# The last six x tiles transposed by DMA, and the loads of the convolution moved behind x

## The chip, the cores and the metric

The kernel runs on the 8 cores of one Trainium2 chip, the same program on each core with its own data. Time is in device microseconds (us) of the slowest core. A core has the engines TensorE (PE), VectorE (DVE), ScalarE (ACT), GpSimd (POOL) and SyncE (SP), and 16 DMA engines. DMAs are issued here from SP (queue q1 of the profile) and from POOL (queue q0).

## The reference, cut to what matters

One layer of a hybrid convolutional decoder, for 8 prompt sequences of 2048 tokens and 128 short sample sequences of 8 tokens; a core gets one prompt sequence and 16 samples, 2176 tokens in all.

```
u = rmsnorm(h) * g_mix
a_b, a_c, a_h, a_z, b_v, b_g, b_z, gate_a, gate_b = split(u @ w_in)      # 9 blocks of 1024 columns
ya = (a_b * dwconv3(a_c * a_h) * silu(a_z)) @ w_out_a
v  = b_v * sigmoid(b_g)
c  = dwconv31(history ++ v) + bias                                       # samples carry 30 rows of history
yb = (silu(layernorm(c)) * silu(b_z)) @ w_out_b
h  = h + (sigmoid(gate_a) * ya + sigmoid(gate_b) * yb) @ w_o
h  = h + sigmoid(rmsnorm(h) * g_ple @ w_pg) * (p @ w_pe)
y  = rmsnorm(h) * g_final
```

## The kernel before, in words

Each engine's instruction stream is written out by hand: `Sched.add` takes an operation with what it reads and writes and puts it at the end of its engine's stream; semaphore waits follow from the reads and writes. So an engine, and a DMA queue's issuer too, goes through its list in program order, and an operation whose input is late holds up all that stand behind it. `pdma` issues a DMA from POOL (it can cast f32 to bf16) and lets six be under way: the seventh waits until the first has landed. `sdma` issues from SP.

Stage 1 brings x in as 17 tiles of 128 tokens (tile index 0 is the samples, 1 to 16 the prompt; six buffers `x1`, four buffers `xb1`). For a tile `s1_a1` squares and sums a row on ACT (its unused product goes into `xb1`) and makes the factor `rsd` with two small operations on POOL; `s1_a2` scales the tile into `xb1` on ACT (line 484); `s1_b` turns it by 8 PE transposes into PSUM (line 498) and copies that on DVE, times g_mix, into `uT` (line 503). Step i of `s1_step` is `s1_b(i)`, `s1_a2(i+1)`, `s1_a1(i+2)`.

Stage 2 is woven with it: `s2_proj(j, si, o, n)` computes channel block j of the GLU for n tokens from `uT` (16 matmuls, line 409; sigmoid on ACT, line 528; product on DVE, line 535) and stores v rows to the DRAM scratch `vd`. The list `PIECES` runs blocks j = 0 to 3 over pieces of the tokens; the flags of a piece say after which j a step of stage 1 stands. The last piece, (3, 0, 512), reads tiles 13 to 16; the piece (2, 256, 256) reads tiles 11 and 12. After the last piece the eight weight buffers (`ring`) come free pair by pair, and POOL loads the weights of j = 4 to 7 into them. Blocks 4 to 7 then run as 20 jobs, the first being j = 4 on the samples.

Between those jobs stand the 16 halves of the convolution (`conv_half`, 20 matmuls each, line 604; halves 2j and 2j+1 belong to block j). A half needs its weights `Wp`, built on DVE from the taps `tw` and a `mask` (`w_build`, line 588), and the window `v8`: prompt rows loaded back from `vd` (`conv_load`, on SP), the history of the samples (`hist_load`, on POOL, one load per j) and their new rows (`vs_load` from `vsd`, then a DVE copy in `conv_samples`, line 580). `v8` has two buffers, so `conv_load(j + 2)` waits for the second half of j.

The rest (branch A, the output projections, the merge, and the per-tile stage 6 with its DMA transposes on SP, line 860) is not changed, except for `s6_tail`, which computes the last two tiles in pieces: `sig` (ACT, line 936) writes the gate into buffer `B`, `comb` (DVE) multiplies and adds, `sqr` (ACT, line 954) squares and sums into the unused half of `yt`, `out` scales and stores.

Of the kernel before, what the change touches and what calls it, by code (L numbers as in the profile page):

```python
# [7 lines left out]
F32 = mybir.dt.float32  # L8
# [4 lines left out]
D = 1024  # L13
# [143 lines left out]
def build_program():  # L157
# [11 lines left out]
    h8_d = din("h8", [NCH, 128, NQ, 80])  # L169
# [10 lines left out]
    gple_d = din("gple", [128, D])  # L180
    gfin_d = din("gfin", [128, D])
# [12 lines left out]
    with contextlib.ExitStack() as st:  # L194
# [50 lines left out]
        wo_t = at("wo_t", [128, NCH, D], BF16, o_acc)  # L245
        NRING = 8
# [41 lines left out]
        xb1 = [at(f"xb1{i}", [128, D], BF16, o_r4 + 4096 * NXS + 2048 * i) for i in range(NXB)]  # L288
        X1_RES = [f"x1{i}" for i in range(NXS)] + [f"xb1{h}{i}" for i in range(NXB) for h in ("", "h")]
# [149 lines left out]

        xnext = [0]  # L440
# [49 lines left out]
        def s1_b(i):  # L490
            t = TILES[i]
# [417 lines left out]
        def s6_tail(t):  # L909
# [3 lines left out]
            gb, eb, cc = {}, {}, {}  # L913

# [18 lines left out]
            def sig(t, i):  # L933
                (o, n), b, x = parts[t][i], gb[t, i], t % 2
                rs_ap, rs_res = s6[t]
                S.add("act", lambda e: e.activation(out=B[x][:, o:o + n], in_=ps[:, b, 0:n], func=AF.Sigmoid, scale=rs_ap),
                      reads=[f"ps{b}", rs_res], writes=[f"B{x}h{i}"])

            def comb(t, i):
                (o, n), b, x, w = parts[t][i], eb[t, parts[t][i][0] // 512], t % 2, t % 4  # L940
                S.add("dve", lambda e: e.tensor_tensor(out=B[x][:, o:o + n], in0=ps[:, b, o % 512:o % 512 + n],
                                                       in1=B[x][:, o:o + n], op=ALU.mult),
                      reads=[f"ps{b}", f"B{x}h{i}"], writes=[f"B{x}h{i}"])
                S.add("dve", lambda e: e.tensor_tensor(out=B[x][:, o:o + n], in0=B[x][:, o:o + n], in1=A[w][:, o:o + n],
                                                       op=ALU.add),
                      reads=[f"B{x}h{i}", f"A{w}"], writes=[f"B{x}h{i}"])

            def sqr(t, i):
                (o, n), x = parts[t][i], t % 2
                if t not in cc:  # L950
# [3 lines left out]
                S.add("act", lambda e: e.activation(out=yt[x][:, o:o + n], in_=B[x][:, o:o + n], func=AF.Square,  # L954
                                                    accum_out=ssq[:, c:c + 1]),
                      reads=[f"B{x}h{i}"], writes=[f"yt{x}h{i}", f"ssq{c}"])
# [9 lines left out]
            def out(t):  # L966
                x, c = t % 2, cc[t] + len(parts[t]) - 1
                for h in range(2):
# [18 lines left out]
            halves_of(ta % 2)  # L987
# [8 lines left out]
            halves_of(tb % 2)  # L996
# [23 lines left out]
        def s1_step():  # L1020
            i = nxt[0]
            if i < len(TILES):
                nxt[0] += 1
                s1_b(i)
                s1_a2(i + 1)
                s1_a1(i + 2)
# [20 lines left out]
        for f, i in FIRST:  # L1047
# [4 lines left out]
            else:  # L1052
# [3 lines left out]
        PIECES += [(1, 0, 256, (1, 0, 1, 0)), (1, 256, 256, (1, 1, 1, 0)), (2, 0, 256, (1, 1, 0, 1)),  # L1056
                   (2, 256, 256, (1, 0, 1, 0)), (3, 0, 512, (0, 0, 0, 0))]
        builds = [(0, 0), (0, 1), (1, 0)]
        for p, (si, o, n, prep) in enumerate(PIECES):
            for j in range(4):  # L1060
# [7 lines left out]
                if si == 3 and o == 0 and builds:  # L1068
                    w_build(*builds.pop(0))
                if si == 2 and o == 0 and j < 2:  # L1070
                    hist_load(j)
                    vs_load(j)
            if p == 0:
# [8 lines left out]
                sdma(hista[:], sa_d, [], ["hista"], "hista")  # L1082
        S.alias([f"cq{q}_{g}" for q in range(4, 8) for g in range(NQ)] + [f"c{q}_4" for q in range(4, 8)], X1_RES)

# [54 lines left out]
        conv_samples(7)  # L1139
        s3_job(0, 3)  # L1140
# [181 lines left out]
```

How the kernel before makes its waits and increments, by code:

```python
            def run(engname, e):  # L113
                waited = {}
                for o in ops:
                    if o["eng"] != engname:
                        continue
                    need = {}
                    for d in o["deps"]:
                        od = ops[d]
                        v = od["seq"] * (16 if od["dma"] is not None else 1)
                        if v > need.get(od["chan"], 0):
                            need[od["chan"]] = v
                    for c, v in need.items():
                        if waited.get(c, 0) >= v:
                            continue
                        e.wait_ge(sems[c], v)
                        waited[c] = v
                    ins = o["fn"](e)
                    if o["signal"]:
                        ins.then_inc(sems[o["chan"]], 16 if o["dma"] is not None else 1)
                if engname == final_wait_eng:
                    for c, v in final.items():
                        if waited.get(c, 0) < v:
                            e.wait_ge(sems[c], v)
```

## Time and profile before

| | |
|---|---|
| median of 3 runs | 882.98 us (882.97 to 884.48) |
| the profiled execution: its time, and the span from first to last instruction on the slowest core | 885.41 us, 882.6 us |
| spans of the 8 cores | 877.8 to 882.6 us |
| mean granted TensorE clock, by core | 0.992 to 0.995 of full speed |
| busy share of the span: PE, DVE, ACT, POOL | 97%, 58%, 34%, 16% |

The profile is of the slowest core, number 3. Busy time of PE is modelled from pipelined matmuls, so a gap in it is read from the start times of groups. Times of events are from the start of the span.

### The profile page before, as it was taken

The numbers are of one execution on the slowest core, as the hardware profiler recorded it, in microseconds if no ns is written. First come the engines' busy times: TensorE is split into PE (matmuls) and PEld (weight loads), VectorE is DVE, ScalarE is ACT, GpSimd is POOL, SyncE is SP. The second block draws the span as 40 slices with busy tenths as digits, with TensorE's granted clock in tenths as the row PEclk, the third lists the DMA queues.
The fourth block names the chain that finished last, engine by engine and source line by source line (L and its number), as shares of the span: only waits on it lengthen the run. The fifth ranks groups of instructions, "written<-read, shape, count | busy, mean of one in ns | idle before, by whom it ended". The sixth has DMA issues, their size and how long they took to land.

```text
span 882.4 us, 15282 instructions; the slowest of 8 cores (877.8 to 882.6 us)
## 1 busy us (share of the span) xinstructions
PE 854.6 (97%) x4970; PEld 441.6 (50%) x4970; DVE 509.0 (58%) x794; ACT 301.9 (34%) x568; POOL 146.1 (17%) x275
## 2 busy tenths in 40 slices
PE   7999999999999999999999999999999999999993
PEld 4886555555454444454454544444444444444441
DVE  2455234576997777777677732333233325777775
ACT  4773224355443232423323321111111112444443
POOL 3242101100101101020110101110001001344442
PEclk9999999999999999999999999999999999999997
DMA  9987899996203213030413276522222145766642
GB/s 190 258 154 98 160 184 176 151 155 116 49 1 48 38 24 61 13 61 1 61 15 59 33 147 96 86 38 46 49 49 33 22 83 129 196 182 170 172 127 98
DMA packets 94108, 84.42 MB, mean 96 GB/s; under 512 B 53296, under 2 KB 74800, under 8 KB 93488
## 3 DMA queue, kind: packets, MB, share of 16 engines
q0 software_dynamic: 27776, 31.17, 25.3%
q1 hardware_dynamic: 66256, 52.29, 24.9%
q8 instruction: 41, 0.67, 0.3%
q14 instruction: 35, 0.29, 0.1%
HBM read 86.80 MB, written 15.61 MB: 116 GB/s over the span
## 4 chain that ended last, share of the span: by engine, by line
PE 85%; DMA 7%; issue 2%; DVE 2%; ACT 2%; POOL 1%; DVEq 0%; POOLq 0%; SPq 0%; ACTq 0%
PE ps L409 65%; PE ps L849 7%; PE ps L870 6%; PE ps L604 4%; DMA t_v<-vd 3%; DMA t_x<-x 2%; PE ps L876 1%; DMA vd<-t_vrow 1%; PE ps L672 1%; DMA t_ring<-w_in 1%; ACT t_xb L424 1%; ACT t_xb L484 1%; DVE t_tmp L714 1%; PE ps L498 0%; PE ps L919 0%
## 5 line engine op out<-in xcount | busy, mean ns | idle before, releaser
L409 PE MATMUL ps<-t_uT,t_ring 128*128 128x512 bf16 (+2 forms) x3200 | 542.6, 329 | 1.5 <-DMA t_ring<-w_in 0.7
L409 PEld LDWEIGHTS ps<-t_uT,t_ring 128*128 128x128 bf16 x3200 | 278.2, 98 | 253.5 <-issue 4.3
L823 DVE TENSOR_TENSOR t_tmp<-ps,t_tmp 128x512 f32<-128x512 f32 (+1 forms) x80 | 48.7, 611 | 151.2 <-PE ps L409 150.6
L343 POOL DMA_DIRECT2D t_ring<-w_in x72 | 39.0, 543 | 391.2 <-PE ps L409 388.3
L820 ACT ACTIVATE t_tmp<-ps 128x512 f32<-128x512 f32 (+1 forms) x80 | 42.3, 532 | 177.2 <-PE ps L409 177.2
L781 ACT ACTIVATE t_tmp<-t_tmp,t_vid 128x512 f32<-128x512 f32 (+1 forms) x40 | 30.0, 749 | 124.0 <-DVE t_tmp L778 124.0
L535 DVE TENSOR_TENSOR t_vrow<-ps,t_tmp 128x512 bf16<-128x512 f32 (+2 forms) x52 | 25.2, 485 | 80.8 <-PE ps L409 38.1
L409 PE MATMUL ps<-t_cb,t_ring 128*128 128x512 bf16 (+1 forms) x320 | 65.4, 347 | 0.0
L409 PE MATMUL ps<-t_yaT,t_ring 128*128 128x512 bf16 (+1 forms) x320 | 65.4, 347 | 0.0
L849 PE MATMUL ps<-t_wo_t,t_cb 128*128 128x512 bf16 x272 | 61.5, 379 | 0.0
L870 PE MATMUL ps<-t_wpg_t,t_u2T 128*128 128x512 bf16 x240 | 54.3, 379 | 0.0
L604 PE MATMUL ps<-t_v,t_Wp 128*128 128x336 bf16 x320 | 48.0, 306 | 4.3 <-DMA t_v<-vd 3.3
L714 DVE SCALAR_TENSOR_TENSOR t_tmp<-t_sx,t_vid,t_tmp 128x512 f32<-128x512 f32 x64 | 48.1, 751 | 6.7
L426 POOL TENSOR_SCALAR t_msq<-t_ssq 128x1 f32<-128x1 f32 x49 | 22.7, 464 | 132.5 <-ACT t_yt L424 50.0
L409 PEld LDWEIGHTS ps<-t_yaT,t_ring 128*128 128x128 bf16 x320 | 29.0, 98 | 30.2
L409 PEld LDWEIGHTS ps<-t_cb,t_ring 128*128 128x128 bf16 x320 | 28.9, 98 | 30.2 <-issue 0.3
L743 DVE TENSOR_TENSOR t_sx<-ps,t_tmp 128x512 f32<-128x512 f32 x32 | 22.1, 690 | 36.1 <-ACT t_tmp L735 31.6
L849 PEld LDWEIGHTS ps<-t_wo_t,t_cb 128*128 128x128 bf16 x272 | 26.6, 98 | 31.8
L604 PEld LDWEIGHTS ps<-t_v,t_Wp 128*128 128x128 bf16 x320 | 31.0, 98 | 21.2 <-issue 5.6
L870 PEld LDWEIGHTS ps<-t_wpg_t,t_u2T 128*128 128x128 bf16 x240 | 23.5, 98 | 28.3
L528 ACT ACTIVATE t_tmp<-ps 128x128 f32<-128x128 f32 (+2 forms) x60 | 23.4, 405 | 36.5 <-PE ps L409 36.3
L611 ACT ACTIVATE t_c<-ps 128x512 f32<-128x512 f32 x32 | 19.0, 596 | 46.2 <-PE ps L604 46.2
(99 smaller groups left out, 764.1 us busy)
## 6 DMA issues: line engine op xcount, KB each, us to landing
t_ring<-w_in POOLq DMA_DIRECT2D x72, 256.0 KB, 6.5
t_x<-x SPq DMA_DIRECT2D x17, 512.0 KB, 8.8
t_xs<-x SPq DMA_DIRECT2D x17, 512.0 KB, 4.7
t_cb<-t_c SPq DMA_DIRECT2D x64, 128.0 KB, 5.1
y<-t_yt SPq DMA_DIRECT2D x15, 512.0 KB, 3.2
vd<-t_vrow SPq DMA_DIRECT2D x28, 128.0 KB, 5.4
t_v<-vd SPq DMA_DIRECT2D x7, 512.0 KB, 7.0
t_ring<-w_oa POOLq DMA_DIRECT2D x8, 256.0 KB, 8.0
```

Of the source, the lines that this page charges most:

```text
L343: S.add("pool", lambda e: e.dma_start(out=out, in_=in_), reads=reads, writes=list(writes) + [swq()], dma=key)
L409: S.add("pe", lambda e, k=k: e.matmul(ps[:, b, 0:n], lhsT=ring[k_ring][:, k, :], rhs=rhs_fn(k), start=(k == 0), stop=(k == NCH - 1)), read ...
L426: S.add("pool", lambda e: e.tensor_scalar(out=msq[:, c:c + 1], in0=ssq[:, c:c + 1], scalar1=1.0 / D, scalar2=EPS, op0=ALU.mult, op1=ALU.ad ...
L528: S.add("act", lambda e: e.activation(out=tmp[tg][:, 0:n], in_=ps[:, bg, 0:n], func=AF.Sigmoid), reads=[f"ps{bg}"], writes=[f"tmp{tg}"])
L535: S.add("dve", lambda e: e.tensor_tensor(out=vst[q][:, o:o + n], in0=ps[:, bv, 0:n], in1=tmp[tg][:, 0:n], op=ALU.mult), reads=[f"ps{bv}", ...
L604: S.add("pe", lambda e, b=b, qq=qq, q=q, d=d: e.matmul(ps[:, b, 0:NWIN], lhsT=Wp[w][:, qq * NLAG + d, :], rhs=v8[s][:, q, 4 - d:4 - d + NWIN],
L714: S.add("dve", lambda e, k=k: e.scalar_tensor_tensor(out=tmp[t2][:, 0:n], in0=tp[k], scalar=vecs[:, V_WCA + 3 * j + k:V_WCA + 3 * j + k + ...
L781: S.add("act", lambda e: e.activation(out=tmp[tx][:, 0:n], in_=tmp[tx][:, 0:n], func=AF.Silu, scale=vcol(V_LNG, j), bias=vcol(V_LNB, j)), ...
L820: S.add("act", lambda e, p=p, t=t: e.activation(out=tmp[t][:, 0:n], in_=ps[:, p, 0:n], func=AF.Sigmoid), reads=[f"ps{p}"], writes=[f"tmp{t}"])
L823: S.add("dve", lambda e, p=p, t=t: e.tensor_tensor(out=tmp[t][:, 0:n], in0=ps[:, p, 0:n], in1=tmp[t][:, 0:n], op=ALU.mult), reads=[f"ps{p} ...
L849: S.add("pe", lambda e, h=h, b=b, k=k: e.matmul(ps[:, b, :], lhsT=cbb[:, k, mcol:mcol + 128], rhs=wo_t[:, k, 512 * h:512 * h + 512], start ...
L870: S.add("pe", lambda e, h=h, b=b, k=k: e.matmul(ps[:, b, :], lhsT=u2T[t % 3][:, k, :], rhs=wpg_t[:, k, 512 * h:512 * h + 512], start=(k == ...
```

## The change

Tiles 11 to 16 of x are no longer turned by PE: DVE scales them with `rsd` and with g_mix (a new input, held as a full row tile `gmix` in the space of the later sums) into `xb1`, and a DMA transpose from SP writes `uT`. For the other tiles stage 1 stays. The sample stores, `mask` and `tw` leave the first piece and stand on POOL behind the fourth; the histories of all j come in one load of 1 MB (after the cast) into `hst`, issued just ahead of them, and `conv_samples` copies a block's part into `v8` on DVE. `hst` lies partly under the `xb1` buffers 1 to 3 (`HST_UNDER`), so its load waits for their last transposes. The steps of stage 1 move forward by some blocks. In the tail the last tile gets other buffers for `B` and for the squares.

```diff
+        FIRST_DT = 11
...
         def s1_a2(i):
...
+            if i >= FIRST_DT:
+                t = TILES[i]
+                si, o = t // 4, 128 * (t % 4)
+                S.add("dve", lambda e: e.scalar_tensor_tensor(
+                    out=xb1[bq][:], in0=xs1[xq][:], scalar=rs_ap, in1=gmix[:], op0=ALU.mult, op1=ALU.mult),
+                    reads=[f"x1{xq}", rs_res, "gmix"], writes=[f"xb1{bq}", f"xb1h{bq}"])
+                if xnext[0] < len(TILES):
+                    s1_load(xnext[0])
+                S.add("sp", lambda e: e.dma_start_transpose(out=uT[si][:, :, o:o + 128], in_=xb1[bq][:]),
+                      reads=[f"xb1{bq}", f"xb1h{bq}"], writes=[f"uT{t}", f"uTh{t}"], dma=f"uT{bq}")
+                return
...
+            if i == 6:
+                sdma(gmix[:], gmix_d, [], ["gmix"], "gmix")
 
         def s1_b(i):
+            if i >= FIRST_DT:
+                return
...
-        def hist_load(j):
-            s = j % 2
-            pdma(v8[s][:, :, 260:340], h8_d[j], [], [f"v8{s}h"], f"v8{s}h")
+        def hist_load():
+            S.alias(["hst"], HST_UNDER)
+            pdma(hst.rearrange("p j q s b -> p (j q s b)"), h8_d, [], ["hst"], "hst")
 
         def conv_load(j):
             s = j % 2
-            if j >= 2:
-                hist_load(j)
...
         def conv_samples(j):
             s = j % 2
+            S.add("dve", lambda e: e.tensor_copy(
+                out=v8[s][:, :, 260:340].rearrange("p q (s b) -> p q s b", b=5)[:, :, :, 0:4], in_=hst[:, j]),
+                reads=["hst"], writes=[f"v8{s}h"])
...
+            qb, qj = tb % 3, (tb + 1) % 3
+            Bt = {ta: (B[ta % 2], f"B{ta % 2}"), tb: (xs[qb], f"xs{qb}")}
+            junk = {ta: (yt[ta % 2], f"yt{ta % 2}"), tb: (xs[qj], f"xs{qj}")}
...
-        PIECES += [(1, 0, 256, (1, 0, 1, 0)), (1, 256, 256, (1, 1, 1, 0)), (2, 0, 256, (1, 1, 0, 1)),
-                   (2, 256, 256, (1, 0, 1, 0)), (3, 0, 512, (0, 0, 0, 0))]
+        PIECES += [(1, 0, 256, (1, 0, 1, 0)), (1, 256, 256, (1, 1, 1, 1)), (2, 0, 256, (1, 1, 1, 0)),
+                   (2, 256, 256, (0, 0, 0, 0)), (3, 0, 512, (0, 0, 0, 0))]
...
-                if si == 3 and o == 0 and builds:
+                if si == 3 and j > 0 and builds:
                     w_build(*builds.pop(0))
-                if si == 2 and o == 0 and j < 2:
-                    hist_load(j)
+                if si == 3 and 1 <= j < 3:
+                    j -= 1
                     vs_load(j)
+            if p == 3:
+                hist_load()
+            if p == 3:
+                for j in range(4):
+                    vsd_store(j)
+                pdma(mask[:], mask_d, [], ["mask"], "mask")
+                pdma(tw.rearrange("p a b -> p (a b)"), tw_d, [], ["tw"], "tw")
             if p == 0:
...
-                for j in range(4):
-                    vsd_store(j)
-                pdma(mask[:], mask_d, [], ["mask"], "mask")
-                pdma(tw.rearrange("p a b -> p (a b)"), tw_d, [], ["tw"], "tw")
                 sdma(hista[:], sa_d, [], ["hista"], "hista")
...
-        h8 = hist.reshape(16, 5, NPH, NCH, NQ, 16).transpose(3, 5, 2, 4, 0, 1)
-        m["h8"] = f(h8.reshape(NCH, 128, NQ, 80))
+        h8 = hist[:, 0:32].reshape(16, 4, NPH, NCH, NQ, 16).transpose(5, 2, 3, 4, 0, 1)
+        m["h8"] = f(h8.reshape(128, NCH * NQ * 64))
```

## Rows read from the trace of the kernel before

**Rows 1.** Busy time by stretch (us, PE, PEld, DVE, ACT, POOL, PEclk, DMA share, GB/s).

```profile
55.00:73.00 18.00, 17.07 (x177) 15.18 (x178) 9.83 (x22) 13.43 (x25) 5.53 (x12) 1.00 0.75 92
...
120.00:127.00 7.00, 4.42 (x20) 2.50 (x20) 2.16 (x3) 0.69 (x2) 0.00 (x0) 0.76 1.55 141
...
206.00:860.00 654.00, 653.71 (x3444) 314.01 (x3442) 401.69 (x600) 199.18 (x352) 100.78 (x177) 1.00 0.36 73
```

**Rows 2.** Timeline of PE, 52 to 97 us (start us, us, what, idle before).

```profile
52.67 1.91 PE L409 MATMUL ps<-t_uT,t_ring 128*128 128x256 bf16 x16
...
61.96 0.61 PE L498 MATMUL ps<-t_idb,t_xb 128*128 128x128 bf16 x8 [0.47 <-ACT t_xb L484]
62.40 3.66 PE L409 MATMUL ps<-t_uT,t_ring 128*128 128x256 bf16 x32
...
72.90 23.52 PE L409 MATMUL ps<-t_uT,t_ring 128*128 128x256 bf16 x128
```

**Rows 3.** Timeline of PE, the three convolution halves that waited.

```profile
97.30 3.02 PE L604 MATMUL ps<-t_v,t_Wp 128*128 128x336 bf16 x20 [0.88 <-DMA t_v<-vd]
...
122.72 4.65 PE L604 MATMUL ps<-t_v,t_Wp 128*128 128x336 bf16 x20 [2.58 <-DMA t_v<-vd]
...
172.06 3.02 PE L604 MATMUL ps<-t_v,t_Wp 128*128 128x336 bf16 x20 [0.99 <-DVE t_vkeep_s L549]
```

**Rows 4.** Timeline of ACT in the tail.

```profile
868.70 1.42 ACT L936 ACTIVATE t_B<-ps,t_rsd 128x512 f32<-128x512 f32 x3 [0.58 <-DVE t_yt L904]
871.32 0.63 ACT L954 ACTIVATE t_yt<-t_B 128x512 f32<-128x512 f32 x1 [1.20 <-DMA y<-t_yt]
```

**Rows 5.** Groups of DVE by line and shape, 20 to 80 us.

```profile
L503 DVE TENSOR_TENSOR t_uT<-ps,t_vid 128x1024 bf16<-128x1024 bf16 x14 | 17.0, 1217 | 0.1
```

**Rows 6.** Timeline of DVE and of POOL, 849 to 853 us.

```profile
851.05 1.28 DVE L904 SCALAR_TENSOR_TENSOR t_yt<-t_B,t_rsd,t_gfin 128x1024 f32<-128x1024 f32 x1
...
849.47 0.18 POOL L426 TENSOR_SCALAR t_msq<-t_ssq 128x1 f32<-128x1 f32 x1 [3.28 <-ACT t_yt L424]
...
851.19 1.19 POOL L426 TENSOR_SCALAR t_msq<-t_ssq 128x1 f32<-128x1 f32 x1 [0.83 <-ACT t_xs L424]
```

**Rows 7.** Line 860, the DMA transposes of stage 6.

```profile
L860 SPq DMA_TRANSPOSE t_u2T<-t_xb x17: 1222/1224/1351, 734.6 to 859.0; - x17
...
DMA to landing us min/median/max: 2.8/2.8/4.6
```

**Rows 8.** Page, DMA issues of x (KB each, median us to landing).

```profile
t_x<-x SPq DMA_DIRECT2D x17, 512.0 KB, 8.7
```

**Rows 9.** Timeline of POOL, 49 to 78 us.

```profile
49.58 2.19 POOL L343 DMA_DIRECT2D vsd<-t_vkeep_s  x4
...
77.16 0.62 POOL L343 DMA_DIRECT2D t_ring<-w_in  x1 [6.68 <-PE ps L409]
```

**Rows 10.** DMA view, 690 to 740 us (KB each, median us to landing).

```profile
t_wpg_t<-w_pg POOLq DMA_DIRECT2D x2, 1024.0 KB, 13.0
```

**Rows 11.** DMA view, 48 to 53 us.

```profile
t_tw<-tw POOLq DMA_DIRECT2D x1, 640.0 KB, 10.3
```

**Rows 12.** DMA view, 76 to 78 us.

```profile
t_ring<-w_in POOLq DMA_DIRECT2D x1, 256.0 KB, 4.0
```

**Rows 13.** DMA view, 83 to 86 us.

```profile
t_ring<-w_in POOLq DMA_DIRECT2D x2, 256.0 KB, 8.7
t_v<-vd SPq DMA_DIRECT2D x1, 512.0 KB, 12.1
```

**Rows 14.** DMA view, 63 to 70 us (packets, MB, share of 16 engines).

```profile
q0 software_dynamic: 1805, 0.29, 61.7%
...
t_v<-h POOLq DMA_DIRECT2D x2, 160.0 KB, 4.2
```

**Rows 15.** DMA view, 109 to 110 us.

```profile
t_v<-vd SPq DMA_DIRECT2D x1, 512.0 KB, 13.1
```

**Rows 16.** Timeline of DVE, 171 to 172 us.

```profile
171.57 0.34 DVE L580 COPY t_v<-t_vs 128x128 bf16<-128x128 bf16 x1
```

More of the change, by code:

```diff
@@ L168, in build_program @@
     sa_d = din("sa", [128, NCH, 32])
-    h8_d = din("h8", [NCH, 128, NQ, 80])
+    h8_d = din("h8", [128, NCH * NQ * 64])
     sbh_d = din("sbh", [352, D])
@@ L180, in build_program @@
     gple_d = din("gple", [128, D])
+    gmix_d = din("gmix", [128, D])
     gfin_d = din("gfin", [128, D])
@@ L245, in build_program @@
         wo_t = at("wo_t", [128, NCH, D], BF16, o_acc)
+        gmix = at("gmix", [128, D], F32, o_acc)
         NRING = 8
@@ L288, in build_program @@
         xb1 = [at(f"xb1{i}", [128, D], BF16, o_r4 + 4096 * NXS + 2048 * i) for i in range(NXB)]
+        hst = at("hst", [128, NCH, NQ, 16, 4], BF16, o_cb + NCH * NTOK * 4 - NCH * NQ * 128)
+        assert o_cb + NCH * NTOK * 4 - NCH * NQ * 128 >= o_r4 + 4096 * NXS + 2048
+        HST_UNDER = [f"xb1{h}{i}" for i in range(1, NXB) for h in ("", "h")]
         X1_RES = [f"x1{i}" for i in range(NXS)] + [f"xb1{h}{i}" for i in range(NXB) for h in ("", "h")]
@@ L953, in sqr @@
                 c, last = cc[t] + i, i == len(parts[t]) - 1
-                S.add("act", lambda e: e.activation(out=yt[x][:, o:o + n], in_=B[x][:, o:o + n], func=AF.Square,
+                S.add("act", lambda e: e.activation(out=jt[:, o:o + n], in_=bt[:, o:o + n], func=AF.Square,
                                                     accum_out=ssq[:, c:c + 1]),
-                      reads=[f"B{x}h{i}"], writes=[f"yt{x}h{i}", f"ssq{c}"])
+                      reads=[f"{br}h{i}"], writes=[f"{jr}h{i}", f"ssq{c}"])
                 S.add("pool", lambda e: e.tensor_scalar(
@@ L971, in out, with halves_of @@
                     S.add("dve", lambda e, hs=hs: e.scalar_tensor_tensor(
-                        out=yt[x][:, hs], in0=B[x][:, hs], scalar=rsd[:, c:c + 1], in1=gfin[:, hs],
+                        out=yt[x][:, hs], in0=bt[:, hs], scalar=rsd[:, c:c + 1], in1=gfin[:, hs],
                         op0=ALU.mult, op1=ALU.mult),
-                        reads=[f"B{x}h{i}" for i in ii] + [f"rsd{c}", "gfin"], writes=[f"yt{x}h{i}" for i in ii])
+                        reads=[f"{br}h{i}" for i in ii] + [f"rsd{c}", "gfin"], writes=[f"yt{x}h{i}" for i in ii])
                     sdma(y_d[128 * t:128 * t + 128, hs], yt[x][:, hs], [f"yt{x}h{i}" for i in ii], [], f"yl{t % 2}{h}")
-            def halves_of(x):
-                S.alias([f"B{x}h{i}" for i in range(3)], [f"B{x}"])
-                S.alias([f"yt{x}h{i}" for i in range(3)], [f"yt{x}"])
+            def halves_of(*names):
+                for nm in names:
+                    S.alias([f"{nm}h{i}" for i in range(3)], [nm])
             gates(ta, 0)
@@ L986, in s6_tail @@
             gates(tb, 1)
-            halves_of(ta % 2)
+            halves_of(f"B{ta % 2}", f"yt{ta % 2}", f"xs{qb}", f"xs{qj}")
             sig(ta, 0)
@@ L995, in s6_tail @@
             s6_out(ta - 1)
-            halves_of(tb % 2)
+            halves_of(f"yt{tb % 2}")
             sqr(ta, 0)
@@ L1021, in s1_step @@
             i = nxt[0]
[L1022 to L1026, printed above, removed]
+            nxt[0] += 1
+            s1_b(i)
+            s1_a2(i + 1)
+            s1_a1(i + 2)
         def s1_load5():
@@ L1077, in build_program @@
                     S.add("pool", lambda e, i=i: e.memset(v8[i][:, :, 0:4], 0.0), writes=[f"v8{i}z"])
-                for j in range(4):
-                    vsd_store(j)
-                pdma(mask[:], mask_d, [], ["mask"], "mask")
-                pdma(tw.rearrange("p a b -> p (a b)"), tw_d, [], ["tw"], "tw")
                 sdma(hista[:], sa_d, [], ["hista"], "hista")
+        assert nxt[0] == len(TILES) - 1
         S.alias([f"cq{q}_{g}" for q in range(4, 8) for g in range(NQ)] + [f"c{q}_4" for q in range(4, 8)], X1_RES)
+        S.alias([f"acc{c}{si}" for c in "sq" for si in range(5)], ["gmix"])
         jobs = [(j, si) for j in range(4, 8) for si in (4, 0, 1, 2, 3)]
@@ L1139, in build_program @@
         conv_samples(7)
+        S.alias([f"cq7_{g}" for g in range(NQ)] + ["c7_4"], ["hst"])
         s3_job(0, 3)
@@ L1275 @@
     shared = dict(w_in=cols(w_in[0]), w_oa=cols(w_out_a[0]), w_ob=cols(w_out_b[0]), w_o=rows(w_o[0]),
-                  w_pg=rows(w_pg[0]), w_pe=rows(w_pe[0]), tw=tw, mask=mask, vecs=vecs, gfin=gfin, gple=gple)
+                  w_pg=rows(w_pg[0]), w_pe=rows(w_pe[0]), tw=tw, mask=mask, vecs=vecs, gfin=gfin, gple=gple, gmix=gmix)
     def phases(a):
```

23 lines of the change are left out of this document (12 added, 11 removed).

## The prediction

> **What bounds the kernel now.** I read the busy time by stretch first, then PE's own timeline, then the DMA view of the stretches where PE stands still. From 206 to 860 us PE is busy 653.71 of 654 us [rows 1], and the change touches nothing there. So the change can only work before 206 us, and in the tail.
>
> Up to 73 us PE loses time to stage 1. Between 52.67 and 72.90 it runs nine blocks of 16 matmuls; two blocks in a row last 3.66 us and one 1.91, so a further one costs 1.75 and nine cost 15.75 [rows 2]. The other 4.5 us of the 20.2 are the transposes of tiles 11 to 16 (0.61 us each, of which some 0.15 overlaps the next block) and the gaps ahead of them, such as the 0.47 us in which PE waits for ACT's scaling [rows 2]. The piece (3, 0, 512) starts at 72.90 + 1.75 = 74.65.
>
> From 97 to 206 us PE waits three times [rows 3]: at 97.30 (0.88 us, half 0, its prompt rows from `vd`), at 122.72 (2.58 us, half 4, the same load of j = 2) and at 172.06 (0.99 us, half 10, behind DVE). The second wait costs more than it lasts: its 20 matmuls take 4.65 us where 20 others take 3.02, and the stretch 120 to 127 us has a granted clock of 0.76 [rows 1, 3], which means that part of it ran at 1.2 instead of 2.4 GHz, after PE had stood still. The shorter two cost no clock. The DMA engines are fully taken there: their share is 1.55 [rows 1].
>
> **Part 1, transposes: 4.5 us.** PE loses 48 transposes and no longer waits for them, if `uT` is there in time. DVE trades six copies of 1.217 us [rows 5] for six scalings of two f32 rows into bf16; the nearest row, the same operation at the same size, has 1.28 [rows 6]: +0.4 us in all, hidden since DVE is busy 9.83 of 18 us there [rows 1]. ACT loses six scalings and its loop with POOL. The new chain is square (ACT), two POOL operations, scaling (DVE), transpose (SP). DVE does one scaling and one block's product per step, estimated at 1.9 us a step, from about 54 us: tile 10's copy, 1.2 us [rows 5], begins when its transposes end, at 52.7. The six scalings then end at 55.9, 57.8, 59.7, 61.6, 63.5 and 65.4. A transpose lands 2.8 us after its issue, at most 4.6 [rows 7]; it occupies SP for 1.22 us, and only stores of v stand behind it there, for which nobody waits yet. Tile 12 is there at 60.6 and needed at 52.67 + 6 x 1.75 = 63.2; tile 16 is there at 68.2 and needed at 63.2 + 7.0 = 70.2. The squares of tiles 15 and 16 wait for the transposes of 11 and 12 (one `xb1` buffer); these land at 58.7 and 60.6, in time for scalings at 61.6 and 63.5. So the last piece starts at 70.2 instead of 74.65. With the landing at 4.6 throughout, tile 16 comes some 1 to 2 us late; the gain is between 2.5 and 4.5 us, and I take 4.5, as the median of 17 transposes is the lowest of them.
>
> One detail: the POOL operation that makes a factor took 0.18 us alone and 1.19 us when it started under a 1.28 us DVE scaling of the same kind [rows 6]. The Trainium skill has a rule for this (SBUF — State Buffer, section "Who interferes with whom"): a DVE operation with two SBUF inputs and a GpSimd operation that reads SBUF share a port pair, and the second waits for the whole of the first. By it each new scaling can put up to 1.2 us into the next tile's chain; the trace agrees. All of it in one tile would use up 1.2 of the 2 us that tile 16 has to spare, so the sum stays and only the chance of late transposes grows.
>
> **Part 2, POOL's queue before the last piece.** Leaving the first piece, the four sample stores free POOL of 2.19 us [rows 9]. They, `mask` and `tw` now stand behind `hist_load`, which waits for tile 15's transpose, about 66.3 us. Two loads of 1 MB issued together land after 13.0 us [rows 10]: 6.1 us per MB and about 1.3 more. So `hst` lands at 66.3 + 7.4 = 73.7. `tw` is the seventh POOL DMA and waits for it; 640 KB make 5.1 us at that pace, against 10.3 measured with x traffic beside it [rows 11]: 79 to 84. Behind `tw` stand the weights of j = 4. Two of 256 KB take 3.2 us at that pace, so they land at about 82 to 87. PE wants them at 70.2 plus four blocks of twice 1.75, which is 84.2. Before, the first was issued at 77.16 and landed in 4.0 us [rows 9, 12], 7 us before PE came. I take no wait, since x is over by then and the idle-queue pace is nearer; at the other end PE waits 3 us and loses some 1.6 us of clock. DVE also stands at the first `w_build` until `tw` lands; behind it are two blocks' products, and PE has free PSUM banks for two jobs more.
>
> **Part 3, half 0: -0.6 us.** PE would come to half 0 two such blocks and a quarter later, at 92.1. Its prompt rows are stored after block (3, j = 0), now 4.5 us earlier; before, the load came 12.1 us after its issue, beside weight loads that took 8.7 [rows 13]. The same eight weight loads run beside it now, and `vs_load(0)` has moved behind it on SP's queue, and the DVE copy behind that. I take a wait of 1.5 us in place of 0.88: bounds 0 and 3 us.
>
> **Part 4, half 4: +3.8 us.** Two history loads of 0.29 MB in total, 1805 packets, take 61.7% of 16 engines over 7 us [rows 14]: 2.2 us each. One such load stood on POOL just ahead of, and another behind, the load of `vd` for j = 2, which landed after 13.1 us [rows 15]. Without the first it should land some 2.2 us sooner. The wait of 2.58 shrinks to 0.4, like those that cost no clock, and the 1.63 us of slow matmuls go too: 2.2 + 1.6 = 3.8. Bounds: 0, if SP's issue and the stores are what delays the load, and 4.2.
>
> **Part 5, half 10: -0.6 us.** DVE's sample copy ends at 171.9, just before PE goes on at 172.06 [rows 3, 16]. Ahead of it now stands the history copy: 512 elements a partition, between 0.34 us (the copy of 128, [rows 16]) and 1.217 (1024 elements, [rows 5]). I take 0.6, all of it on PE's path. The other seven copies lie beside DVE idle time.
>
> **Part 6, tail: +0.5 us.** The last tile's gate waits 0.58 us for DVE to read the shared `B`, and its square waits 1.20 for the store of `yt` [rows 4]. With other buffers ACT starts the gate when its previous square ends, 0.5 us sooner, and DVE's chain behind it moves along; the second wait lies within the same stretch and brings no more. Bounds 0.3 and 0.8.
>
> **The sum.** 4.5 - 0.6 + 3.8 - 0.6 + 0.5 = 7.6 us. The profiled execution took 885.41 us, with a span of 882.6; the runs' median is 882.98, 2.4 us less, and I take the sum from it: **875.4 us**.
>
> **Rivals.**
> *The weights come late* (the other side: slower). `hst` and `tw` stand ahead of the weights of j = 4. At the slowest rows for each step, `hst` 13.0, `tw` 10.3, weights 8.7 us [rows 10, 11, 13], they land at 66.3 + 32.0 = 98.3 instead of 84.2. PE then waits 14.1 us and loses 1.6 of clock; half 0's extra wait vanishes. 875.4 + 15.7 - 0.6 gives 890.5. It decides against the change from a landing at about 91 us on, when the wait has eaten the 7.6 us. For it: six DMAs at once, and some 1.8 MB ahead of the weights that were not there before. Against it: those rows all had other traffic beside them.
> *The transposes come late.* In this stage x took 8.7 us to land [rows 8]. With that for a transpose, tile 12 comes at 66.5 (3.3 us late), tile 16's square waits for it, its scaling ends about 70 and it lands about 78.8: the last piece starts 8.6 us later than I say, and the clock may fall by another 1.6: 884 to 885.6 us. Against: the 17 transposes of stage 6, with loads of x and stores of y beside them, needed 4.6 at most [rows 7].
> *Half 4 still waits.* If the load of j = 2 is held by SP's stores and not by histories, part 4 is 0: 879.2.
> *All waits go:* 4.5 + 0.9 + 4.2 + 1.0 + 0.6 = 11.2 us: 871.8.
>
> **Chances.** Forecast, within 2.5 us of 875.4: 0.50. Half 4 still waits, or a wait of 2 to 4 us at the weights (878 to 881): 0.22. All waits go: 0.08. Weights late enough to lose all: 0.10. Transposes late: 0.10, of which half ends between 880 and 884. A measurement of this kernel can tell 0.2% (1.8 us) from no change. Faster 0.80, same 0.08, slower 0.12. The range is 871.5 to 882.5; the two late cases lie mostly outside.
>
> **What would show it.** After: no transposes of PE behind 53 us, the last piece near 70 us; j = 4's first job near 84 with no wait on `ring`; half 0 near 93; half 4 with a wait under 1 us and 3.0 us long; half 10 with a wait of 1.6; ACT's gate of the last tile right behind the square. The prediction is wrong if PE waits on `uT` at 63 or 70 us, or on `ring` at 84, or if half 4's rows still land after 13 us.

## The result, and the profile after

The changed kernel took 894.28 us (median of 4 runs, 893.91 to 895.24), the kernel before 883.73 us on the same chip (4 runs): a ratio of 1.012, 95% interval 1.010 to 1.0139. It is slower, by some 10.6 us; 875.4 was forecast. The profiled execution took 893.91 us, with a span of 892.4 on core 0, its slowest; the rows of before are core 3's, its slowest.

PE's timeline on core 0 (start us, us, what, idle ahead of it and what ended it), beside [rows 2] and [rows 3]:

```profile
53.05 17.63 PE L415 MATMUL ps<-t_uT,t_ring 128*128 128x256 bf16 x160
70.98 13.76 PE L415 MATMUL ps<-t_uT,t_ring 128*128 128x512 bf16 x62 [0.30 <-issue]
94.41 1.01 PE L415 MATMUL ps<-t_uT,t_ring 128*128 128x128 bf16 x8 [9.67 <-DMA t_ring<-w_in]
96.93 9.53 PE L415 MATMUL ps<-t_uT,t_ring 128*128 128x128 bf16 x39 [1.50 <-DMA t_ring<-w_in]
109.48 3.02 PE L628 MATMUL ps<-t_v,t_Wp 128*128 128x336 bf16 x20 [3.03 <-DVE t_v L604]
...
132.16 3.02 PE L628 MATMUL ps<-t_v,t_Wp 128*128 128x336 bf16 x20
...
180.53 3.02 PE L628 MATMUL ps<-t_v,t_Wp 128*128 128x336 bf16 x20 [1.66 <-DVE t_vkeep_s L572]
```

Behind 53 us no transposes are left on PE, and the last piece starts at 70.98. Then PE stands for 9.67 and 1.50 us, until the weights of j = 4 land, and for 3.03 us ahead of half 0, which begins at 109.48 where it began at 97.30. Half 4 has no wait left, half 10 waits 1.66 us.

POOL's timeline (its DMA issues, core 0) shows what the weights stood behind:

```profile
69.95 0.60 POOL L349 DMA_DIRECT2D t_hst<-h  x1 [5.20 <-DVE t_vkeep L564]
70.55 2.12 POOL L349 DMA_DIRECT2D vsd<-t_vkeep_s  x4
72.66 0.54 POOL L349 DMA_DIRECT2D t_mask<-mask  x1
82.54 0.54 POOL L349 DMA_DIRECT2D t_tw<-tw  x1 [9.34 <-DMA t_hst<-h]
83.10 2.74 POOL L349 DMA_DIRECT2D t_ring<-w_in  x5
92.01 0.53 POOL L349 DMA_DIRECT2D t_ring<-w_in  x1 [6.17 <-DMA t_tw<-tw]
```

`tw` is the seventh transfer and waits 9.34 us for the histories; the weights, first issued at 77.16 before [rows 9], are issued at 83.10. The DMA view of 82 to 86 us (KB each, median us to landing), beside [rows 12] and [rows 13]:

```profile
t_ring<-w_in POOLq DMA_DIRECT2D x5, 256.0 KB, 14.6
t_tw<-tw POOLq DMA_DIRECT2D x1, 640.0 KB, 8.9
t_v<-vd SPq DMA_DIRECT2D x1, 512.0 KB, 23.2
...
t_vs<-vsd SPq DMA_DIRECT2D x1, 32.0 KB, 24.8
```

The five weight loads took 14.6 us in the median (before, the first alone took 4.0 and the two of 83 us 8.7); the first two of them, for which PE stood, landed 11.1 and 12.9 us after their issue. The prompt rows took 23.2 us (12.1 before), and 32 KB of sample rows, behind them on SP's queue, 24.8. What fills the DMA engines shows in the busy time by stretch, first the kernel before, then the changed one, both on core 0 (us, PE, PEld, DVE, ACT, POOL, PEclk, DMA share, GB/s):

```profile
56.00:72.00 16.00, 15.25 (x157) 13.44 (x155) 9.13 (x19) 12.14 (x22) 5.55 (x12) 1.00 0.79 98
72.00:84.00 12.00, 11.95 (x75) 6.87 (x75) 6.42 (x13) 2.31 (x6) 2.22 (x4) 1.00 0.48 81
84.00:98.00 14.00, 12.78 (x70) 6.14 (x70) 4.75 (x10) 2.67 (x5) 2.66 (x5) 1.00 0.97 168
```

```profile
56.00:72.00 16.00, 15.70 (x140) 13.53 (x139) 10.64 (x25) 6.39 (x15) 5.87 (x12) 1.00 0.94 144
72.00:84.00 12.00, 11.95 (x57) 5.46 (x56) 1.53 (x4) 2.39 (x4) 2.61 (x6) 1.00 0.85 124
84.00:98.00 14.00, 2.83 (x21) 1.89 (x20) 5.64 (x7) 0.28 (x1) 3.36 (x7) 0.62 0.93 144
```

Before, the DMA engines had room (0.79, 0.48) until 84 us; now they have none from 56 us on. PE's granted clock was 0.62 from 84 to 98 us, where it mostly stood. From 56 to 72 us SP's queue alone, which carries the transposes, held them for 91.0% of the time, where it held 16.6% before:

```profile
q1 hardware_dynamic: 7091, 2.26, 91.0%
```

That is 14.6 us against 2.7. Six stores of v were issued there instead of three; if these take the 2.7 us twice, some 9 us are left for six transposes, 1.5 us of all 16 engines each (an estimate). With nothing beside it a transpose takes less: one of stage 6, in the kernel before, held them for 83.0% of the 1.4 us from 735.7 to 737.1, which is 1.16 us. The landing of the six, beside [rows 7]:

```profile
DMA to landing us min/median/max: 3.1/3.8/5.8
```

### The profile page after: what moved, and what is told of

It reads as the page before. It is cut to its first block, busy times and chain, and to the rows that moved or that the text cites. A ratio compares the mean times of both kernels' runs of the same rounds, so it can differ in the third digit from the quotient of the medians.

```text
span 892.4 us, 15095 instructions; the slowest of 8 cores (886.1 to 892.4 us)
## 1 busy us (share of the span) xinstructions
PE 848.8 (95%) x4841; PEld 439.9 (49%) x4922; DVE 511.7 (57%) x802; ACT 296.4 (33%) x562; POOL 137.7 (15%) x268
## 4 chain that ended last, share of the span: by engine, by line
PE 87%; DMA 8%; issue 2%; DVE 1%; ACT 1%; POOL 0%; DVEq 0%; SPq 0%; POOLq 0%; ACTq 0%
PE ps L415 67%; PE ps L873 7%; PE ps L894 6%; PE ps L628 5%; DMA t_vs<-vsd 3%; DMA t_x<-x 3%; DMA t_ring<-w_in 1%; PE ps L900 1%; DMA vd<-t_vrow 1%; PE ps L696 1%; PE ps L946 0%; ACT t_xb L430 0%; PE ps L521 0%; DVE t_accs L667 0%; DVE t_B L968 0%
```

## The experiments

Each ran beside the kernel before on the same chip. Theory A: the order on POOL's queue (`hst`, then `tw`, then the weights) makes the loss. Rivals: B, the megabyte of histories alone; C, the DMA transposes alone; then D and E, that the DMA engines' time runs out. This table is the result in short: ratio to the kernel before, then from PE's timelines the smallest and the largest wait over the eight cores, in us.

| kernel | ratio (95%) | PE waits for transposes | for weights of j = 4 | at half 0 |
|---|---|---|---|---|
| before | 1 | 0 | 0 | 0 to 2.3 |
| changed | 1.0120 (1.0100 to 1.0139) | 0 | 4.5 to 11.2 | 2.4 to 5.1 |
| e1 stores, tw early | 1.0048 (1.0031 to 1.0066) | 2.1 to 4.6 | 0 | 4.3 to 6.6 |
| e2 e1, histories behind weights | 1.0113 (1.0097 to 1.0129) | 1.3 to 2.6 | 0 | 9.4 to 11.1 |
| e3 old histories, stores early | 1.0032 (1.0003 to 1.0060) | 3.6 to 6.2 | 0 | 0 to 0.9 |
| e4 old histories, stores late | 1.0059 (1.0041 to 1.0078) | 2.8 to 6.1 | 0 | 3.5 to 4.9 |
| e5 no DMA transposes | 1.0111 (1.0060 to 1.0163) | 0 | 3.7 to 7.5 | 2.5 to 5.1 |
| e6 histories, tw split | 1.0089 (1.0056 to 1.0121) | 0 to 2.6 | 0 to 4.1 | 5.5 to 14.9 |
| e7 e2, sample rows early | 1.0093 (1.0065 to 1.0121) | 1.4 to 5.4 | 0 | 7.9 to 10.9 |
| e8 tail alone | 0.9989 (0.9967 to 1.0010) | 0 | 0 | 0 to 1.6 |
| e9 before plus 1 MB | 1.0028 (1.0000 to 1.0055) | 0 | 0 | 2.2 to 3.9 |
| e10 one load in conv stretch | 1.0034 (1.0014 to 1.0055) | 0 | 0 | 0 to 4.6 |
| e11 e10, three DMA transposes | 1.0066 (1.0041 to 1.0091) | 2.0 to 4.2 | 0 | 0 to 7.8 |
| e12 e7, no histories | 1.0008 (0.9992 to 1.0024) | 1.6 to 6.0 | 0 | 0 to 2.3 |
| e13 tw ahead of histories | 1.0191 (1.0139 to 1.0243) | 1.1 to 21.2 | 0 to 3.8 | 0.3 to 5.9 |
| e14 small loads | 0.9993 (0.9958 to 1.0028) | 0 to 6.7 | 0 | 0 to 2.5 |
| e15 e14, no DMA transposes | 1.0013 (0.9993 to 1.0033) | 0 | 0 | 0 to 3.9 |
| e16 e14, four DMA transposes | 1.0066 (1.0041 to 1.0092) | 1.2 to 4.7 | 0 | 0 to 3.4 |

### What held the weights: e5, e1, e13

**e5.** All tiles on TensorE again, with the steps of before and without the load of the gain; the rest as changed.

```diff
-        FIRST_DT = 11
+        FIRST_DT = 99
```

> Edit: the changed kernel with all tiles of x transposed on TensorE as before, and without the load of the broadcast gain; the one load of the histories, the late stores, mask and tw, and the tail stay. Theory A (the order on POOL's queue alone sets the loss): the histories land some 12 us after their issue, tw and the weights of j = 4 follow as in the changed kernel, PE waits about 10 us for them, and the 4 us of TensorE's transposes come back on top: 892 to 898 us. Theory D (the time of the 16 DMA engines is what runs out between 56 and 98 us; the queue that carries the transposes holds 91% of them from 56 to 72 us, where the same queue before held 17%): without the transposes the histories land in 8 to 9 us, PE waits 2 to 4 us: 878 to 886 us.

1.0111: as slow as the changed kernel. On core 4:

```profile
73.33 15.72 PE L415 MATMUL ps<-t_uT,t_ring 128*128 128x256 bf16 x80
93.19 0.61 PE L415 MATMUL ps<-t_uT,t_ring 128*128 128x128 bf16 x8 [4.14 <-DMA t_ring<-w_in]
96.34 9.76 PE L415 MATMUL ps<-t_uT,t_ring 128*128 128x128 bf16 x40 [2.54 <-DMA t_ring<-w_in]
```

The first row begins with one block of the piece before (1.75 us), so the last piece starts at 75.08, 4.1 us later than the 70.98 with DMA transposes; the histories were issued at 70.89 us, as in the changed kernel (69.95). Over the eight cores PE asks for the first weights 3.7 us later on average (88.4 against 84.7) and begins with them only 1.1 us later (91.8 against 90.8). So most of what PE gains is waited away, the two times can't be told apart, and rival C falls for this wait. The time is theory A's, the length of the wait is between A and D. The histories took 9.7 to 11.8 us to land, and 10.1 to 12.0 in the changed kernel: without the DMA transposes they were hardly faster.

**e1.** The stores, `mask` and `tw` back behind piece 0.

```diff
             if p == 3:
                 hist_load()
-            if p == 3:
-                for j in range(4):
-                    vsd_store(j)
-                (mask, tw)
             if p == 0:
+                for j in range(4):
+                    vsd_store(j)
+                (mask, tw)
```

> Edit: the changed kernel with the four vsd stores, mask and tw back behind piece 0, ahead of the rest of x; the 1 MB of histories stays where the change puts it, ahead of the last piece. Theory A (tw, held until the histories have landed by the six transfers that POOL may have in flight, holds the weights of j = 4 behind it): the five weight loads are issued from about 75 us, share the queue with the histories, and PE's wait at 84 to 85 us falls from 11.2 us to about 4 or less; 880 to 886 us. Rival B (the megabyte of histories alone delays the weights): hardly less wait, 889 to 894 us. Rival C (the DMA transposes and what SP carries set it): no change, 892 to 895 us.

PE's wait for weights is gone on all cores, with the megabyte still ahead of them. Part of that is hidden, though. The first of the weights landed at 85.3 to 88.4 us (80.3 to 82.5 before, 86.3 to 94.2 in the changed kernel), and PE, itself held by the transposes, asked later; at the changed kernel's 84.7 it would have waited some 1 to 4 us (an estimate). That much is left to rival B, the megabyte alone; the rest of the 4.5 to 11.2 us is not. The time, 889.45 us, is above theory A's range: some 40% of the loss stays, in two new places (core 3):

```profile
66.48 31.56 PE L415 MATMUL ps<-t_uT,t_ring 128*128 128x256 bf16 x176 [3.09 <-DMA t_uT<-t_xb]
...
103.97 5.76 PE L628 MATMUL ps<-t_v,t_Wp 128*128 128x336 bf16 x20 [5.93 <-DVE t_v L604]
```

The transposes come 3.09 us late, and half 0 waits 5.93 us for DVE's copy of sample rows.

**e13.** `tw` ahead of the histories, nothing else.

```diff
-            if p == 3:
-                hist_load()
             if p == 3:
                 for j in range(4):
                     vsd_store(j)
                 (mask, tw)
+                hist_load()
```

> Edit: the changed kernel with the load of all histories behind the four stores, mask and tw, still ahead of the last piece: an exchange of places on POOL's queue and nothing else. If the order alone made the wait (tw held until the histories have landed, and the weights behind tw): tw lands some 9 us after 73 us, and PE's wait for the weights of j = 4 falls from 4.5 to 11.2 us to under 4 us on every core; 882 to 889 us. If the bytes set it, whatever their order: the wait stays over 4 us on most cores, 891 us or more.

The wait for weights fell to 3.8 us and less, as the order alone should do; on two cores, where PE came far too late to need them, that shows nothing, on the other six it does. The time did not fall: 1.0191, the slowest of all. On two cores the last transposes, beside which `tw` and then the histories were issued, came 16.0 and 21.2 us late. Line 499 (the transposes) on one of them, who waited for it and the landing:

```profile
  PE ps L415: 21.2, 1
...
DMA to landing us min/median/max: 3.1/4.7/23.8
```

So theory A names the cause of most of this wait: the same bytes in the other order leave 0 to 3.8 us of it, the histories without `tw` beside them (e1) some 1 to 4, and `tw` late without the histories (e4, below) had the first weights there by 81.7 to 85.0 us. Its cure moves the wait to another transfer.

### What held half 0: e2, e7, e6, e12, e9

**e2.** As e1, with the histories behind the first weights.

```diff
                 if si == 3 and o + n == 512:
                     wdone(s2w[j][0])
+                if si == 3 and j == 0:
+                    hist_load()
```

> Edit: as the experiment with the stores early, and the load of the histories stands behind the first weight loads of j = 4 (after the first job of the last piece). Theory A and rival B both expect that the weights land before PE asks at 84 to 85 us and the wait there is under 1 us: 875 to 880 us, the first conv half may still wait for sample rows up to 3 us. Rival C: still 887 to 895 us.

A clear miss for all: no wait for weights, but 9.4 to 11.1 us at half 0. The DMA view of core 7, 80 to 90 us:

```profile
q0 software_dynamic: 359, 1.16, 87.4%
q1 hardware_dynamic: 140, 0.13, 4.7%
```

POOL's queue has 87.4% of the DMA engines, SP's 4.7%. On SP's stand the stores of v that the rows of half 0 are loaded from (10.3 us to landing in this stretch), then those rows, then the sample rows, for which DVE waits until 108.34.

**e7.** As e2, with `vs_load` at the third piece, as before.

```diff
-                if si == 3 and 1 <= j < 3:
-                    j -= 1
+                if si == 2 and o == 0 and j < 2:
                     vs_load(j)
```

> Edit: as the experiment with the histories behind the weights, and the two loads of sample rows back where the kernel before has them, at the third column piece instead of behind the first load of conv rows. If half 0 waited there for the sample rows alone (19 us to landing behind 512 KB of conv rows): its wait of 9.6 to 11 us falls to 0 to 3 us, 885 to 889 us, the rest of the loss being the transposes that come late (1.3 to 2.6 us on the slow cores) and what follows them. If the histories themselves or the DMA engines' time hold half 0: 892 us or more.

No better: half 0 now waits for the prompt rows themselves, which on core 2 took

```profile
t_v<-vd SPq DMA_DIRECT2D x1, 512.0 KB, 21.2
```

**e6.** A quarter of the histories and of `tw` ahead of the last piece, the rest behind it and behind half 0; both `vs_load` ahead of the first `conv_load`.

```diff
             if p == 3:
-                hist_load()
+                hist_load(0)      # j = 0, 1
...
-                pdma(tw.rearrange("p a b -> p (a b)"), tw_d, [], ["tw"], "tw")
+                tw_load(0)        # j = 0, 1
...
+                if si == 3 and j == 3:
+                    tw_load(1)
...
                 half()
+                if hk[0] == 1:
+                    hist_load(1)
```

> Edit: the changed kernel with the histories of j = 0, 1 (256 KB) ahead of the last piece and the other 768 KB behind the first conv half, tw's part for j = 0, 1 (160 KB) ahead of the last piece and its other 480 KB behind it, and both early loads of sample rows ahead of the first load of conv rows. Theories A and D: 1.2 MB fewer stand ahead of the weights of j = 4; PE's waits at 84 and at 94 us fall to under 2 us together and half 0 waits under 1 us: 873 to 880 us, under both kernels. Where the transposes then come late instead, as in the experiment with the old histories: 882 to 888 us.

A miss too. The weights were nearly in time, the rows of half 0 were not (5.5 to 14.9 us): `vs_load` waits on SP's queue for the late sample stores, and the prompt rows behind it leave later, into the rest of `tw` and the histories.

**e12.** As e7, the histories' tile set to zero instead of loaded, so that their part is missing from the output.

```diff
-            pdma(hst.rearrange("p j q s b -> p (j q s b)"), h8_d, [], ["hst"], "hst")
+            S.add("dve", lambda e: e.memset(hst.rearrange("p j q s b -> p (j q s b)"), 0.0), writes=["hst"])
```

> Edit: as the experiment with the histories behind the weights and the sample rows early, but the histories are not loaded: VectorE sets their tile to zero, so the output lacks their part. Theory E: PE's wait of 8 to 11 us at half 0 falls to under 2 us and the waits for the transposes (1.4 to 5.4 us) stay: 880 to 886 us. If half 0 waits for something else: 891 us or more.

Half 0 waits 0 to 2.3 us instead of 7.9 to 10.9, and the prompt rows take

```profile
t_v<-vd SPq DMA_DIRECT2D x1, 512.0 KB, 14.0
```

on core 2; over the eight cores 7.7 to 14.0 us, against 15.3 to 21.2 in e7. So in e7 the megabyte held them; it cost 0.85% (1.0093 against 1.0008), 7.5 us, give or take 3. Without any history load the kernel is still no faster than before, as the transposes are 1.6 to 6.0 us late.

**e9.** The kernel before with that megabyte added, unread.

```diff
+            if p == 3:
+                hst_load()
```

> Edit: the kernel before with one load added, the megabyte of histories ahead of the last column piece, whose data nothing reads (the histories by j stay and are used). Theory E (the DMA engines' time between the last piece and the first conv half is full: 2 MB of weights and the 512 KB of conv rows fill 97% of it from 84 to 98 us already, and the large packets of POOL's queue take it ahead of SP's): the weights of j = 4 land some 4 us later and the conv rows of half 0 8 to 10 us later; 6 to 11 us slower than before. Theory A in its narrow form (only tw, held until the histories have landed, delayed the weights, and nothing is held here): up to 3 us slower.

0.28%, 2.5 us (0 to 4.9): theory E's price, 6 to 11 us, is wrong for this place, and only its direction is right. Issued at 71 us, into a stretch in which the DMA engines of the kernel before have a share of 0.48, the megabyte landed after 13.1 us (core 6) and cost half 0 about 2 us. The same megabyte costs some three times that behind the weights (e7). Bytes alone don't set the price; what they run beside does, and e7 differs from e9 in more than the place, as its transposes go by DMA.

### What made the transposes late: e3, e4, e14 to e16, e11

**e3.** Only the transposes and the tail; histories, stores, `tw` and sample rows as before.

> Edit: the transposes by DMA and the buffers of the last tile alone; histories by j in the conv stretch, stores, mask and tw early, sample rows at the third column piece, all as in the kernel before. Theory A and rival B: the forecast's terms for half 4 (3.8) and half 10 (0.6) are lost and the rest stays: about 879 to 881 us. Rival C: 887 to 895 us.

1.0032, not faster: PE waits 3.6 to 6.2 us for the transposes, more than the 4 us that they save. From 50 to 56 us all of `tw` is issued (landing 11.5 us), from 56 to 72 two history loads of small packets, and a transpose's landing goes from 3.8 to

```profile
t_uT<-t_xb SPq DMA_TRANSPOSE x5, 5.0
```

as the median of five on core 5, 9.4 at most. The time, 888.5 us, misses what A and B promised and lies in rival C's range: the DMA transposes alone, in the old order, lose what they should gain. With the landings beside it, this is theory D.

**e4.** The changed kernel with the old histories, stores and `tw` still late.

> Edit: the changed kernel with the histories by j in the conv stretch as before, no load of all histories; the four vsd stores, mask and tw stay late, ahead of the last piece. Theory A: tw is issued at about 73 us without the histories to wait for, the weights of j = 4 some 3 to 5 us later than with early stores, PE waits 0 to 4 us: 879 to 885 us. Rival B: as the experiment with the old histories, 879 to 881 us. Rival C: 890 us or more. If instead the late tw alone were enough for the loss, 888 us or more.

1.0059, above theory A's range. No wait for weights, so late `tw` alone does not make it; the transposes are late by 2.8 to 6.1 us, with the small-packet history loads and the stores beside them and `tw` only from 71 us on (they land after 6.0 us in the median on core 0), and half 0 waits 3.5 to 4.9 us for sample rows.

**e14, e15, e16.** Early: stores, `mask`, a quarter of `tw`, sample rows; histories of j = 0, 1 ahead of the last piece; later 128 KB of histories and 80 KB of `tw` for each j. e15 has no DMA transposes, e16 four.

```diff
         def conv_load(j):
+            if j >= 2:
+                hist_load(j, j + 1)
+                if j + 2 < NCH:
+                    tw_load(j + 2, j + 3)
...
             if p == 3:
-                hist_load()
+                hist_load(0, 2)
...
+                if si == 3 and j == 3:
+                    tw_load(2, 4)
```

> Edit: six transposes by DMA and the tail's buffers; stores, mask and a quarter of tw (160 KB) early, sample rows early, the histories of j = 0, 1 (256 KB) ahead of the last piece, another quarter of tw behind it, and then 128 KB of histories and 80 KB of tw for each later j beside its conv rows. If what stood beside the transposes made them late: PE's waits for them fall from 1.4 to 6.2 us to under 2 us, weights and conv rows of half 0 are in time within 2 us, and all of the forecast but a part of half 4 comes: 877 to 882 us. If the transposes are late by themselves: 2 us or more of wait there, 883 to 887 us.

> Edit: as the experiment with small loads, with all tiles of x transposed on TensorE and without the load of the broadcast gain. The twin that tells the worth of the DMA transposes: if they are in time there, this is 2 to 4 us slower than it; if they are late, within 1 us of it. Against the kernel before: no worse than 1 us, up to 4 us faster by the conv stretch.

> Edit: as the experiment with small loads, with the last four tiles of x transposed by DMA instead of six. If six in a row fill the DMA engines: PE's waits for the transposes fall under 2 us on every core, and the time is 1 to 3 us under that of the kernel before. If a single transpose beside other traffic is late already (as with three beside all of tw): waits of 2 to 5 us on some cores, within 2 us of the kernel before.

e14 and e15 cannot be told from the kernel before, nor from each other: the transposes were still late by themselves, as the second branch of e14's expectation has it. In e14 half 0 begins between 92.64 and 102.89 us: two cores hardly waited for transposes (spans 874.7 and 880.0 us), another waited 6.69, and the time is that of the slowest:

```profile
77.54 24.59 PE L415 MATMUL ps<-t_uT,t_ring 128*128 128x512 bf16 x112 [6.69 <-DMA t_uT<-t_xb]
```

Four transposes do worse than six: their tiles come last, their first is issued at 63 to 66 us instead of 56, and the slowest lands after 6.0 to 7.6. With 1.0066 it also missed both of its ranges. So fewer transposes were no cure here, but this run moved them as well and doesn't settle how many would fit.

**e10, e11.** The kernel before with the tail, the histories of j = 2 to 7 in one load behind half 0; e11 adds three DMA transposes, with all of `tw` early.

```diff
                 half()
+                if hk[0] == 1:
+                    hst_load()
```

> Edit: the kernel before with the tail's other buffers, and the histories of j = 2 to 7 in one load of 768 KB issued behind the first conv half, where the stretch of the weights of j = 4 is over; j = 0, 1 by themselves as before; taps, mask, stores and all transposes as before. Theory E: the conv stretch gets the part of the forecast that the changed kernel showed there (half 4 without its wait of up to 2.9 us, half 10 with 0.6 us less) without what it paid ahead of it: 1.5 to 4.5 us faster than before. If the 768 KB then hold the conv rows of j = 1 as the megabyte held those of j = 0: 0 to 6 us slower.

> Edit: as the one load in the conv stretch, and the last three tiles of x (not six) transposed by DMA. Theory E: half of the transposes' DMA time (some 5 us of all 16 engines) fits into the 21% that was free from 56 to 72 us, PE saves some 2 us: 1 to 2.5 us under the experiment with one load in the conv stretch. If any DMA transpose beside tw and the histories comes late, as in the experiment with the old histories: 1 to 4 us over it.

1.0034 and 1.0066: the gains that theory E promised did not come, and both lie in the range of the second branch. In e10 half 4 still waits up to 3.7 us for its prompt rows. The 768 KB had landed before that load was issued, so they don't hold it directly. Its rows land sooner than before, after 9.5 us instead of 11.5 (means of eight cores), about the 2.2 us that part 4 counts on. But on seven cores the load is issued 8.2 to 9.8 us behind the start of half 1 instead of 5.8: on core 3 the four stores of v that stand ahead of it on SP's queue, issued while the 768 KB ran, take 5.47 us to issue instead of 2.37. In e11 three transposes are late by 2.0 to 4.2 us, like six. (The expectations of e10 and e3 count half 10's 0.6 us as a gain; the prediction had it as a cost, and it is one.)

### The tail: e8

> Edit: the kernel before with the other buffers for the last tile and nothing else. The forecast's term: 0.5 us faster than the kernel before on the same chip (0 to 1.0). If the longer end handshake seen in the changed kernel belongs to these buffers, 0 to 0.5 us slower.

0.9989 (0.9967 to 1.0010): 1 us faster within an uncertainty of 2. The traces settle it more closely. From the start of PE's last group of matmuls to the end of the span the eight cores take 16.4 to 16.9 us, 16.8 on average, where they took 17.2 to 17.6, 17.4 on average, before: 0.6 us less, as the forecast's 0.5 has it. In the changed kernel it is 17.1.

## Why the prediction was wrong

**The step that failed** is part 2's "I take no wait", as the rival "the weights come late" had it; three of its terms were mis-sized. The histories were issued at 69.95 us, not 66.3; they landed after 12.0, not 7.4; the two weights that PE needs first landed after 11.1 and 12.9, not 3.2. The prediction took "the idle-queue pace" because x is over by then, and it misread that pace: the 13.0 of [rows 10] is the median of two landings, 10.2 us for the first megabyte and 15.7 for the second, so neither landed after 7.4 there. In no run here did the megabyte of histories land in under 9.7 us, with DMA transposes or without (e5). For `tw` and the weights the stretch was not idle either: stores of v, `tw` and five weight loads run beside one another, and the rows of 83 us [rows 13] were nearer. The rival's sum, 890.5, came within 4 us.

How the 17.4 us between the forecast span (882.6 - 7.6 = 875.0) and the measured one (892.4) arose on core 0: 0.8 from the later start of the last piece, 11.2 from the waits for weights, 3.0 instead of 1.5 at half 0, and some 2.4 from the clock, as the 8 and 39 matmuls behind the waits took 1.01 and 9.53 us where 8 took 0.61 in e5 and 39 took 7.51 in e1. That is 15.9, and half 0 came 15.9 us after the forecast 93.6. The other 1.5 lie behind half 0.

**Part 1** was right in what it said (no transposes on PE, the last piece at 70.98 against 70.2, PE without a wait for `uT`), and only in this arrangement: in e1, e3, e4 and e12, with `tw` or history loads beside them, the transposes are late on every core. It priced the transposes on PE, DVE and SP, and not on the 16 DMA engines, where each takes 1.16 us alone and some 1.5 here. The rival "the transposes come late" was what met nearly every attempt to mend the weights.

**Part 3**: half 0 waits 2.4 to 5.1 us, on six cores above the bound of 3. The load that had "moved behind it on SP's queue", the sample rows, ended last (24.8 us).

**Part 4** was right on the core that it was read from (half 4 at 132.16, no wait, 3.02 long), and worth less on the others. Before, half 4 waited 2.6 to 2.9 us on cores 3 and 5 and 0 to 1.8 us on the other six. From half 1 to half 10 the eight cores took 64.1 to 68.9 us before, 65.7 on average, and 64.7 after on every one. That is 1.0 us less with half 10's extra 0.7 in it, so part 4 is worth some 1.6 us on average (an estimate), where 3.8 were read off the slowest core. From half 0 to the end the average gain is 0.3 us, because half 0 itself runs at the lower clock on four cores (4.4 to 5.8 us instead of 3.0; one core before). The rows of half 4 landed after 5.7 to 9.9 us instead of 10.3 to 13.4, so by more than the 2.2 us of the forecast. The mechanism of part 4, fewer history loads beside the prompt rows, was not tried by itself; e10 comes nearest, with about 2 us.

**Part 5** was right in size: 1.66 us in place of 0.99; the history copy takes 0.34 us, and DVE begins the next copy 0.45 us after that one's start. **Part 6**: the gate runs right behind the square,

```profile
877.80 0.19 ACT L981 ACTIVATION_READ_ACCUMULATOR t_yt<-t_B 128x1 f32 x1
877.89 1.62 ACT L963 ACTIVATE t_xs<-ps,t_rsd 128x512 f32<-128x512 f32 x3
```

and e8's traces show the forecast gain of the part alone, 0.6 us; its times can't, as their interval holds none.

**Open:** why SP's packets got so small a share beside POOL's, and why e13 held the transposes on two cores of eight. In the two rows of e2, POOL's 359 packets carry 1.16 MB, 3.2 KB each on average, SP's 140 carry 0.13 MB, 0.9 KB each. The Trainium skill (DMA: Bandwidth & Descriptors, section "Queues, rings and completion order") says that each DMA engine takes turns between its queues packet by packet; if its packets are those that the profile counts, the queue with the larger ones gets the larger share. The two rows agree with it in direction, but no run here varied the size of packets. And SP's 4.7% is in part want of work: in those 10 us it had one store of 128 KB under way, and the load behind it waits for that store; that the store took 10.3 us (2.9 in the changed kernel from 56 to 72 us) is the plainer sign. No version that ran beats the kernel before by more than its uncertainty; e8 and e14 come nearest.

## What to carry to other kernels

Moving work from TensorE to the DMA engines spends DMA time: before counting the gain, write down the DMA share of the stretch, and what else is due to land there. A load costs by what it runs beside, so a landing time is borrowed from the nearest stretch with the same neighbours, not from an idle queue, and the median of two landings is not the time of both; the same megabyte cost about 2.5 us at one place and 7.5 at another. And a wait read off the slowest core counts only so far as the other seven have it: compare all eight, between two points of the program that hold that wait and little else.

## What the runs showed of the hardware

A DMA transpose of a 128x1024 bf16 tile occupies SP for 1.2 us, lands after 2.8 us at best (stage 6, [rows 7]) and takes 1.16 us of all 16 DMA engines alone; beside loads from POOL the slowest of a core's transposes landed after 4.8 to 9.8 us, and in e13, beside 1.6 MB of them, after 20.1 and 23.8 us on two cores. The load of the 1 MB of histories, with a cast, on POOL's queue took 9.7 us or more on every core of every run that has it. SP's 512 KB of rows for half 0 took 9.9 to 13.2 us before, 20.3 to 24.0 in the changed kernel and up to 28.9 in e6, where the rest of `tw` and the histories were loaded beside them. On every core of the changed kernel a POOL operation that makes a factor took 1.58 us when it began 0.1 us after a new DVE scaling, and 0.55 alone; the Trainium skill's rule on the shared port pair (SBUF — State Buffer, section "Who interferes with whom") agrees, and PE waited for no `uT`. Another one, which began within 0.01 us of a scaling, took 0.55 too.
